# Roundings moved to GpSimd and the late layer-norm squares and variance rearranged, in a decoder layer on one core

## The chip, the core and the metric

The kernel runs on one core of a Trainium2 chip. The metric is the device time of the program in microseconds: the median of three runs. TensorE does matrix products and transposes, VectorE and ScalarE elementwise work and row reductions, GpSimd elementwise work in SBUF and part of the DMA issues, SyncE the other DMA issues. Each engine runs its own list of instructions in order and waits on semaphores for the others.

## The reference

One step of a decoder layer on a prompt of 512 tokens and 8 samples of 4 tokens, all in float32, so 544 tokens of width 1024:

```
h = rms_norm(x, g_pre)
z = h @ w_in          # 1024 x 3072: q 512 | k 256 | v 256 | ga 512 | u 512 | vs 512 | gg 512
att = block-sparse causal attention(q, k, v)     # 8 heads of 64, 4 kv heads; samples also over 1024 cached positions
v_rows = group_layer_norm(gelu(vs), g_sgu)       # 8 groups of 64: (v - mean) * rsqrt(var + 1e-5) * g
gm = gelu(u) * (tril(w_spatial[g]) @ v_rows + b) # inside chunks of 128 positions
y = x + rms_norm(concat(att * silu(ga), gm * silu(gg)) @ w_out, g_post)
```

Outputs are y, the new k and v rows, and v_rows of the samples. The variance of the layer norm is the mean of the squares of v - mean in each group of 64.

## The kernel before

All engines follow one list, `SCHEDULE`, written out by `schedule()`; each engine's program walks the list and does its part of each step. The backbone is the input projection. w_in is cut into 24 tiles of 128 columns, in the order q, k, v, vs, u, ga, gg (tiles 0-3, 4-5, 6-7, 8-11, 12-15, 16-19, 20-23); a tile is done in two halves of tokens (256 and 288), which makes 48 halves, numbered 0 to 47: step `("Z", n, half)`, half number 2n + half from tile 3 on. `("ZE", n, half)` is what is done with the result. `after(h, ...)` hangs other steps behind half h.

A product in float32 is made of three products of split values: hi x hi, hi x lo and lo x hi. A weight tile (`w_raw`, 128x1024) is rounded to its high part by ScalarE (`split_hi`, L845) and its low part, the difference, is made by VectorE or GpSimd (`split_lo`, L1094 or L718; `lo_by` says which: VectorE for tiles 7 to 12 among others). Both are issued ahead of the evacuation of the tile before: `next_split(n, 0)` is tile n + 1. TensorE waits for the high part before a tile's first half (L1541) and for the low part two thirds into it (L1546). Results of halves go alternately to two PSUM banks, and a half can't start before the bank's last result has been taken. GpSimd issues the loads of w_in tiles in pairs (`load_w_in`, L726), once both tiles that lay there have been split.

Steps that the change touches:

- `KVN tt`: TensorE turns v of token tile tt into a PSUM bank `T`; ScalarE takes it to `vn_t` (L856), rounds it to `v_st`, the high part, (L952); VectorE makes the low part (L1211); GpSimd stores `vn_t` (L771). KVN 4 is that of the samples. KVN 4 and 0 hang behind half 16, KVN 1, 2 and 3 behind 17, 20 and 22. So in GpSimd's list KVN 1 comes ahead of the step `("Z", 9, 0)`, half 18, at which tile 10 is split.
- `VSN tt`: TensorE turns gelu(vs) of token tile tt; VectorE takes the group sums (L1308) and subtracts the means (`vn`, L1310), which frees the bank; ScalarE squares (`ln_sq`, L982); VectorE adds up the squares (`ln_var`, L1313). One `ln_sq` serves all tiles in turn. VSN 3 and 4 hang behind halves 28 and 29.
- `DEX 1`: ScalarE's exponentials of the second decode round, eight of 128 columns and `p_own` (L962, L963), behind half 28 and ahead of VSN 3.
- `DOT 0`: TensorE turns the decode output and VectorE copies it in four pieces (L1299). `DPT 1`: transposes of the exponentials in two banks `T`, taken by ScalarE and VectorE (L1282).
- Halves 29, 30 and 31 (of u) have their gelu made by hand: ScalarE squares (L926), VectorE L1141, ScalarE tanh (L987), VectorE L1174 (writes `zu`, frees the bank), GpSimd halves it (L818).
- `LN`, behind half 30: VectorE makes variance + 1e-5 from the sums (L1318), shifts and subtracts for a first guess of the inverse root (L1319, L1320), GpSimd does three Newton steps (L807 to L812). `LNM`, from half 33 on: VectorE multiplies by the root, GpSimd by g_sgu.
- `PSC`, `PN`, `PS`, `PTR`, `PPV`, `ATT` u: the prompt's attention, 16 units, from half 30 on: scores, row maxima (`nmax`, L1334), exponentials (`probs`, L1000), scaling, transposes, product with v. The scores of a unit wait for the exponentials of the unit before it, as they use the same banks.

Of the kernel before, what the change touches and what calls it, by code (L numbers as in the profile page):

```python
# [39 lines left out]
ALU = mybir.AluOpType  # L40
ACT = mybir.ActivationFunctionType
# [16 lines left out]
GRP, GCH = 8, 64  # L58
# [27 lines left out]
def schedule():  # L86
# [4 lines left out]
    def after(n, *steps):  # L91
        side.setdefault(n, []).extend(steps)
# [31 lines left out]
    after(30, ("LN",))  # L124
# [77 lines left out]
def lo_by(n):  # L202

    return "pool" if n in (0, 1, 2, 5, 6) or 13 <= n <= NT else "dve"


def next_split(n, half):

    if (n, half) == (2, 1):
        return 3  # L210
    return n + 1 if half == 0 and n >= 3 else None


# [45 lines left out]
def build(nc, x_prompt, x_sample, cache_k, cache_v, page_table, g_pre, w_in, g_sgu, w_spatial,  # L259
# [13 lines left out]
    with ExitStack() as ctx:  # L273
        def sem(name):
            return ctx.enter_context(nc.semaphore(name))
# [180 lines left out]
        w_hi_done = sem("w_hi_done")  # L456
# [226 lines left out]
        def _(pool):  # L683
# [31 lines left out]
            def split_lo(n):  # L715

                pool.wait_ge(w_hi_done, split_count(n))
                nc.gpsimd.tensor_tensor(w_split_tile(False, n), w_tile(n), w_split_tile(True, n).bitcast(fp32), ALU.subtract)\  # L718
                    .then_inc(w_split["pool"], 1)
# [36 lines left out]
            for s in SCHEDULE:  # L756
# [4 lines left out]
                elif kind == "Z" and next_split(*s[1:]) is not None:  # L761
                    n = next_split(*s[1:])
                    if lo_by(n) == "pool":
                        split_lo(n)
                    if n % 2 and n + 3 < NT:
                        load_w_in((n + 3) // 2)
                elif kind == "KVN":
                    tt = s[1]
                    pool.wait_ge(t_free["act"], freed(T_FREED_BY, T_OF[s])[1])
                    if tt < 4:  # L770
                        pool.dma_start(kv_rows(v_prompt, v_sample, tt), vn_t[:, tt % 2, :]).then_inc(stored_v[tt % 2], 16)  # L771
                    else:
                        pool.dma_start(kv_rows(k_prompt, k_sample, tt), kv_s[:, 0:KVW]).then_inc(stored_kvs, 16)
                        pool.dma_start(kv_rows(v_prompt, v_sample, tt), kv_s[:, KVW:2 * KVW]).then_inc(stored_kvs, 16)
# [27 lines left out]
                elif kind == "LN":  # L802
# [27 lines left out]
        def _(act):  # L830
# [7 lines left out]
            def split_hi(n):  # L838

                w_slot_free(act, n)  # L840
                if n < 2:
                    act.wait_ge(w_first[n], 16)
                else:
                    act.wait_ge((w_in_p if w_by_pool(n) else w_in_s)[n // 2 % 2], w_load_count(n))
                nc.scalar.activation(w_split_tile(True, n), w_tile(n), ACT.Copy).then_inc(w_hi_done, 1)  # L845

            def x_stats(tt):
                R = ROWS[tt]
                act.wait_ge(x_in[tt], 16)
                link(nc.scalar.activation(x_sq[0:R, :], x_sb[0:R, tt, :], ACT.Square, accum_out=x_ss[0:R, tt:tt + 1]))  # L850
                nc.scalar.activation(x_sd[0:R, tt:tt + 1], x_ss[0:R, tt:tt + 1], ACT.Sqrt, scale=1.0 / D, bias=RMS_EPS).then_inc(x_std, 1)

# [10 lines left out]
            for s in SCHEDULE:  # L863
# [19 lines left out]
                elif kind == "Z":  # L883
# [3 lines left out]
                    if next_split(n, half) is not None:  # L887
                        split_hi(next_split(n, half))
# [51 lines left out]
                elif kind == "KVN":  # L940
# [9 lines left out]
                    if tt < 4:  # L950
                        act.wait_ge(t_free["act"], freed(T_FREED_BY, n)[1])
                        nc.scalar.activation(v_st[:, tt, :, 0:HD], vn_t[:, tt % 2, :].rearrange("p (h d) -> p h d", h=KVH), ACT.Copy)\  # L952
                            .then_inc(vst_hi, 1)
                elif kind == "DEX":
# [5 lines left out]
                    for n in range(8):  # L960
                        cs = slice(n * P, (n + 1) * P)
                        nc.scalar.activation(pd[:, cs], S[:, cs], ACT.Exp, bias=bbias[:, n // 2, n % 2:n % 2 + 1])  # L962
                    nc.scalar.activation(p_own[:, :], own_s[:, r, :], ACT.Exp, bias=nm_d).then_inc(d_exp, 1)  # L963
# [8 lines left out]
                elif kind == "VSN":  # L972
                    tt = s[1]
                    R = ROWS[tt]
                    act.wait_ge(t_free["dve"], freed(T_FREED_BY, T_OF[s])[1])
                    if tt:
                        act.wait_ge(ssq_done, tt)
                    else:
                        for n in range(2):
                            act.wait_ge(stored_v[n], 2 * 16)  # L980
                        act.wait_ge(vst_done, 4)
                    nc.scalar.activation(ln_sq[0:R, :], vn[0:R, tt, :], ACT.Square).then_inc(sq_done, 1)  # L982
# [100 lines left out]
        def _(dve):  # L1083
# [8 lines left out]
            def split_lo(n):  # L1092
                dve.wait_ge(w_hi_done, split_count(n))
                nc.vector.tensor_tensor(w_split_tile(False, n), w_tile(n), w_split_tile(True, n).bitcast(fp32), ALU.subtract)\  # L1094
                    .then_inc(w_split["dve"], 1)
# [20 lines left out]
            for s in SCHEDULE:  # L1116
# [197 lines left out]
                elif kind == "LN":  # L1314
                    dve.wait_ge(ln_made, 1)
                    dve.wait_ge(ssq_done, TT)
                    var, std, r = (t[:, :, :].rearrange("p t g -> p (t g)") for t in (ln_var, ln_std, ln_rstd))
                    link(nc.vector.tensor_scalar(var, var, 1.0 / GCH, LN_EPS, ALU.mult, ALU.add))  # L1318
# [136 lines left out]
        def _(pe):  # L1455
# [47 lines left out]
            for s in SCHEDULE:  # L1503
# [4 lines left out]
                elif kind == "Z":  # L1508
# [31 lines left out]
                    if half == 0:  # L1540
                        pe.wait_ge(w_hi_done, split_count(t))  # L1541
# [238 lines left out]
```

## Time and profile before

| | us |
|---|---|
| median of 3 runs | 280.27 (280.08 to 280.91) |
| profiled execution, its own time | 280.61 |
| its span, first to last instruction | 278.9 |
| TensorE busy | 270.3 (97%) |
| VectorE busy | 193.3 (69%) |
| ScalarE busy | 161.1 (58%) |
| GpSimd busy | 90.6 (32%) |

Busy time of TensorE is that of its matmuls, whose ends are modelled and overlap: a matmul starts before the one ahead of it ends by the record. Its clock is given as a share of full speed. In the chain of work that ended last TensorE has 82%, VectorE 8% and ScalarE 6%. Times in the text are us from the start of the span.

### The profile page before, as it was taken

How to read it: one execution, taken by the hardware profiler on the slowest of the kernel's cores; microseconds unless marked ns; L12 is line 12 of the kernel's file. 1: busy time of each engine (PE TensorE's matmuls, PEld its weight loads, DVE VectorE, ACT ScalarE, POOL GpSimd, SP SyncE). 2: the span in 40 equal slices, each digit the busy share in tenths (PEclk: the TensorE clock that was granted, in tenths of full speed). 3: DMA queues.
4: the chain of work that ended last, by engine and by line, in shares of the span. 5: the costliest groups of instructions: out<-in, count | busy, mean ns of one | idle time of the engine just before them, and what ended most of it. 6: DMA issues, size and time to landing. Idle time of an engine off the chain costs nothing.

```text
span 278.9 us, 6188 instructions
## 1 busy us (share of the span) xinstructions
PE 270.3 (97%) x2147; PEld 236.9 (85%) x2147; DVE 193.3 (69%) x460; ACT 161.1 (58%) x382; POOL 90.6 (32%) x116
## 2 busy tenths in 40 slices
PE   8999999999999999998999999999999999999992
PEld 3799998998997887997777999999998976767892
DVE  4796896699744545948756777877867794917772
ACT  5973569532692323184576587797786663628621
POOL 4576505210302042142762965443350510000000
PEclk9999999999999999999999999999999999999997
DMA  7989995469799979404464218004008404040043
GB/s 245 336 264 202 203 255 119 150 205 260 215 297 285 280 223 312 153 0 153 129 186 151 51 27 249 19 0 152 0 23 302 152 0 150 5 148 0 21 180 121
DMA packets 29986, 43.39 MB, mean 156 GB/s; under 512 B 3027, under 2 KB 22483, under 8 KB 29956
## 3 DMA queue, kind: packets, MB, share of 16 engines
q1 hardware_dynamic: 26226, 29.76, 37.7%
q0 software_dynamic: 3728, 13.24, 15.4%
q8 instruction: 17, 0.28, 0.5%
q14 instruction: 13, 0.11, 0.1%
q10 hardware_dynamic: 2, 0.00, 0.0%
HBM read 39.59 MB, written 3.41 MB: 154 GB/s over the span
## 4 chain that ended last, share of the span: by engine, by line
PE 82%; DVE 8%; ACT 6%; issue 2%; DVEq 0%; POOL 0%; ACTq 0%; POOLq 0%
PE Z L1543 12%; PE Z L1548 12%; PE Z L1544 12%; PE T L1460 5%; PE O L1684 4%; PE S L1585 3%; PE O L1620 2%; PE Z L1498 2%; PE S L1657 2%; PE S L1498 2%; PE S L1499 2%; PE Z L1500 2%; PE S L1500 2%; PE Z L1499 2%; PE S L1658 2%
## 5 line engine op out<-in xcount | busy, mean ns | idle before, releaser
L1543 PE MATMUL Z<-act_hi,w_hi 128*128 128x288 f32 (+1 forms) x344 | 89.8, 294 | 0.8 <-DVE zu L1174 0.4
L1544 PE MATMUL Z<-act_lo,w_hi 128*128 128x288 f32 (+1 forms) x344 | 88.1, 288 | 0.0
L1543 PEld LDWEIGHTS Z<-act_hi,w_hi 128*128 128x128 f32 x344 | 64.8, 188 | 3.1 <-issue 1.6
L1544 PEld LDWEIGHTS Z<-act_lo,w_hi 128*128 128x128 f32 x344 | 64.8, 188 | 0.0
L718 POOL TENSOR_TENSOR w_lo<-w_raw,w_hi 128x1024 fp32r<-128x1024 f32 x16 | 38.3, 2395 | 46.2 <-ACT w_hi L845 46.1
L1548 PE MATMUL Z<-act_hi,w_lo 128*128 128x256 f32 (+1 forms) x336 | 49.0, 288 | 0.2 <-DVE w_lo L1094 0.2
L1548 PEld LDWEIGHTS Z<-act_hi,w_lo 128*128 128x128 f32 x336 | 44.8, 188 | 0.4 <-DVE w_lo L1094 0.4
L845 ACT ACTIVATE w_hi<-w_raw 128x1024 fp32r<-128x1024 f32 x32 | 33.5, 1050 | 15.0 <-DMA w_raw<-in_w_out 9.8
L1094 DVE TENSOR_TENSOR w_lo<-w_raw,w_hi 128x1024 fp32r<-128x1024 f32 x15 | 18.9, 1268 | 16.1 <-ACT w_hi L845 16.1
L1000 ACT ACTIVATE probs<-S,nmax 128x128 f32<-128x128 f32 (+3 forms) x32 | 16.6, 524 | 21.0 <-DVE nmax L1334 20.2
L726 POOL DMA_DIRECT2D w_raw<-in_w_in x10 | 9.4, 936 | 33.1 <-DVE w_lo L1094 29.4
L1218 DVE STREAM_TRANSPOSE kT<-k_ring 128x1024 f32<-128x1024 f32 x16 | 19.8, 1236 | 0.4 <-PE S L1585 0.3
L1334 DVE TENSOR_REDUCE nmax<-S 128x1 f32<-128x128 f32 (+3 forms) x32 | 14.1, 484 | 4.4 <-PE S L1660 4.4
L1009 ACT ACTIVATE probs<-probs,rsum 128x128 f32<-128x128 f32 (+3 forms) x32 | 16.4, 573 | 0.0
L1347 DVE TENSOR_TENSOR pT_lo<-T,pT_hi 128x128 fp32r<-128x128 f32 (+3 forms) x32 | 14.2, 485 | 1.4 <-ACT pT_hi L1019 0.9
L1356 DVE TENSOR_TENSOR O<-O,o_tmp 64x128 f32<-64x128 f32 x32 | 9.5, 296 | 6.9 <-ACT o_tmp L1027 6.2
L1019 ACT ACTIVATE pT_hi<-T 128x128 fp32r<-128x128 f32 (+3 forms) x32 | 12.2, 440 | 0.5 <-PE T L1460 0.5
L1460 PE MATMUL T<-ident,probs 128*128 128x128 f32 x80 | 12.2, 278 | 0.0
L826 POOL TENSOR_TENSOR zu<-zu,zgg 128x544 f32<-128x544 f32 x4 | 5.4, 1355 | 20.5 <-DVE zgg L1185 20.5
L1684 PE MATMUL O<-pT_hi,v_st 128*128 128x256 f32 x40 | 11.6, 316 | 0.0
L922 ACT ACTIVATE zvs<-Z 128x256 f32<-128x256 f32 (+1 forms) x8 | 3.1, 398 | 13.8 <-PE Z L1548 13.8
L1657 PE MATMUL S<-k_hi,q_st 128*128 128x256 f32 (+2 forms) x32 | 10.8, 347 | 0.3 <-ACT probs L1000 0.3
(281 smaller groups left out, 561.1 us busy)
## 6 DMA issues: line engine op xcount, KB each, us to landing
w_raw<-in_w_in POOLq DMA_DIRECT2D x10, 1024.0 KB, 7.8
k_ring<-in_cache_k SPq DMA_DIRECT2D x64, 128.0 KB, 4.6
v_ring<-in_cache_v SPq DMA_DIRECT2D x64, 128.0 KB, 3.4
w_raw<-in_w_out SPq DMA_DIRECT2D x8, 512.0 KB, 4.3
x_sb<-in_x_prompt SPq DMA_DIRECT2D x4, 512.0 KB, 4.7
x_res<-in_x_prompt SPq DMA_DIRECT2D x4, 512.0 KB, 5.3
out<-y_sb SPq DMA_DIRECT2D x8, 256.0 KB, 2.0
w_raw<-in_w_in SPq DMA_DIRECT2D x2, 512.0 KB, 6.5
```

The lines of the kernel that those rows point to most:

```text
L718: nc.gpsimd.tensor_tensor(w_split_tile(False, n), w_tile(n), w_split_tile(True, n).bitcast(fp32), ALU.subtract)\
L845: nc.scalar.activation(w_split_tile(True, n), w_tile(n), ACT.Copy).then_inc(w_hi_done, 1)
L1000: ins = nc.scalar.activation(probs[:, u % 2, g, 0:keys], S[:, g * 512:g * 512 + keys], ACT.Exp, bias=nmax[:, u % 2, g:g + 1], accum_out=ps ...
L1009: nc.scalar.activation(part, part, ACT.Copy, scale=rsum[:, u % 2, g:g + 1]).then_inc(p_norm[g], 1)
L1094: nc.vector.tensor_tensor(w_split_tile(False, n), w_tile(n), w_split_tile(True, n).bitcast(fp32), ALU.subtract)\
L1218: nc.vector.transpose(kT[:, m // 2 % 2, m % 2, :, :, :].rearrange("p q a j -> p (q a j)"), k_slot(m).rearrange("p q c -> p (q c)")).then_i ...
L1460: return nc.tensor.transpose(T[n % 2][0:out_rows, col:col + rows], in_, ident[0:rows, 0:rows])
L1543: mm(out, wh[:, k, :], act_hi[:, k, cols], start=(k == 0), stop=False)
L1544: mm(out, wh[:, k, :], act_lo[:, k, cols], start=False, stop=False)
L1548: last = mm(out, wl[:, k, :], act_hi[:, k, cols], start=False, stop=(k == KD - 1))
L1657: mm(out, q, k_hi[:, kvh, 0:keys], start=True, stop=False)
L1684: last = mm(O[o_bank(u)][:, 0:256], v_st[:, j, kvh, :], part[:, u % 2, j, :, :].rearrange("p g q -> p (g q)"), start=(j == 0 and e == 0), ...
```

## The change

Five edits:

1. The rounding of v to `v_st` (step KVN) is made by GpSimd, ahead of its store, and no more by ScalarE.
2. The high part of weight tile 10 is made by GpSimd, where it splits ahead of half 18's step; VectorE's low part of that tile and TensorE wait for it. The semaphore `w_hi_done` becomes two, one for each maker, with counts by `hi_count`.
3. The square of VSN 3 is issued by ScalarE after the third of the eight exponentials of DEX 1. The others stay where they were.
4. Variance + 1e-5 is made by GpSimd (step LNV, behind half 30), no more by VectorE.
5. The guess by VectorE and the Newton steps by GpSimd (step LNG) hang behind half 31.

```diff
-    after(30, ("LN",))
+    after(30, ("LNV",))
+    after(31, ("LNG",))
+def hi_by(n):
+    return "pool" if n == 10 else "act"
+def hi_count(n):
+    return sum(hi_by(m) == hi_by(n) for m in SPLIT_ORDER[:split_count(n)])
-        w_hi_done = sem("w_hi_done")
+        w_hi_done = {"act": sem("w_hi_done_act"), "pool": sem("w_hi_done_pool")}
...
# GpSimd
                     n = next_split(*s[1:])
+                    if hi_by(n) == "pool":
+                        w_slot_free(pool, n)
+                        pool.wait_ge(w_in_p[n // 2 % 2], w_load_count(n))
+                        nc.gpsimd.tensor_copy(w_split_tile(True, n), w_tile(n)).then_inc(w_hi_done["pool"], 1)
                     if lo_by(n) == "pool":
                         split_lo(n)
...
                     if tt < 4:
+                        nc.gpsimd.tensor_copy(v_st[:, tt, :, 0:HD], vn_t[:, tt % 2, :].rearrange("p (h d) -> p h d", h=KVH)).then_inc(vst_hi, 1)
                         pool.dma_start(kv_rows(v_prompt, v_sample, tt), vn_t[:, tt % 2, :]).then_inc(stored_v[tt % 2], 16)
...
-                elif kind == "LN":
+                elif kind == "LNV":
+                    pool.wait_ge(ssq_done, TT)
+                    var = ln_var[:, :, :].rearrange("p t g -> p (t g)")
+                    nc.gpsimd.tensor_scalar(var, var, 1.0 / GCH, LN_EPS, ALU.mult, ALU.add).then_inc(ln_made, 1)
+                elif kind == "LNG":
                     pool.wait_ge(ln_guess, 1)
...
# ScalarE
+            def ln_square(tt):
+                R = ROWS[tt]
+                act.wait_ge(t_free["dve"], freed(T_FREED_BY, T_OF["VSN", tt])[1])
+                if tt:
+                    act.wait_ge(ssq_done, tt)
...
+                nc.scalar.activation(ln_sq[0:R, :], vn[0:R, tt, :], ACT.Square).then_inc(sq_done, 1)
...
-                    if tt < 4:
-                        act.wait_ge(t_free["act"], freed(T_FREED_BY, n)[1])
-                        nc.scalar.activation(v_st[:, tt, :, 0:HD], vn_t[:, tt % 2, :].rearrange("p (h d) -> p h d", h=KVH), ACT.Copy)\
-                            .then_inc(vst_hi, 1)
...
                         nc.scalar.activation(pd[:, cs], S[:, cs], ACT.Exp, bias=bbias[:, n // 2, n % 2:n % 2 + 1])
+                        if r and n == 2:
+                            ln_square(3)
...
-                elif kind == "VSN":
...
+                elif kind == "VSN" and s[1] != 3:
+                    ln_square(s[1])
...
# VectorE
-                elif kind == "LN":
-                    dve.wait_ge(ln_made, 1)
-                    dve.wait_ge(ssq_done, TT)
+                elif kind == "LNG":
+                    dve.wait_ge(ln_made, 2)
                     var, std, r = (t[:, :, :].rearrange("p t g -> p (t g)") for t in (ln_var, ln_std, ln_rstd))
-                    link(nc.vector.tensor_scalar(var, var, 1.0 / GCH, LN_EPS, ALU.mult, ALU.add))
                     link(nc.vector.tensor_scalar(std.bitcast(i32), var.bitcast(i32), 1, None, ALU.logical_shift_right))
```

## Rows read from the trace of the kernel before

**Rows 1.** Busy us of each engine by stretch, granted clock, DMA share, GB/s.

```profile
124.00:142.00 18.00, 16.46 (x143) 13.86 (x142) 11.78 (x33) 10.27 (x31) 9.85 (x18) 1.00 0.41 126
...
142.00:226.00 84.00, 84.00 (x720) 77.18 (x719) 64.09 (x202) 61.61 (x162) 39.57 (x31) 1.00 0.33 105
```

**Rows 2.** Timeline, TensorE: start, us, line, operation, [idle before <-releaser].

```profile
82.49 0.39 PE L1543 MATMUL Z<-act_hi,w_hi 128*128 128x256 f32 x1 [0.34 <-ACT zvs L922]
...
128.70 0.66 PE L1460 MATMUL T<-ident,pd 128*128 128x128 f32 x4 [0.91 <-DVE vn L1310]
...
130.43 0.40 PE L1543 MATMUL Z<-act_hi,w_hi 128*128 128x288 f32 x1 [0.37 <-DVE zu L1174]
...
135.18 0.39 PE L1657 MATMUL S<-k_hi,q_st 128*128 128x256 f32 x1 [0.26 <-ACT probs L1000]
```

**Rows 3.** Timeline, ScalarE, from 122 us.

```profile
122.48 2.18 ACT L962 ACTIVATE pd<-S,bbias 128x128 f32<-128x128 f32 x8
...
124.71 0.68 ACT L982 ACTIVATE ln_sq<-vn 128x512 f32<-128x512 f32 x1
125.23 0.46 ACT L926 ACTIVATE gelu_t<-Z 128x288 f32<-128x288 f32 x1
```

**Rows 4.** Timeline, VectorE, from 125 us.

```profile
125.42 0.69 DVE L1313 TENSOR_REDUCE ln_var<-ln_sq 128x8 f32<-128x512 f32 x1 [3.28 <-ACT ln_sq L982]
...
126.89 0.46 DVE L1141 SCALAR_TENSOR_TENSOR gelu_t<-gelu_t,Z 128x288 f32<-128x288 f32 x1
...
127.97 0.68 DVE L1310 SCALAR_TENSOR_TENSOR vn<-ln_mu,T 32x512 f32<-32x512 f32 x1
...
129.95 0.43 DVE L1174 SCALAR_TENSOR_TENSOR zu<-gelu_t,Z 128x288 f32<-128x288 f32 x1
...
131.83 2.11 DVE L1318 TENSOR_SCALAR ln_var<-ln_var 128x40 f32<-128x40 f32 x1
...
134.29 0.48 DVE L1334 TENSOR_REDUCE nmax<-S 128x1 f32<-128x128 f32 x2
```

**Rows 5.** Timeline: two tensor-scalars of VectorE, and GpSimd's low parts beside L1241 and L1318.

```profile
66.61 0.22 DVE L1241 TENSOR_SCALAR st<-off,stat 128x4 f32<-128x4 f32 x1
...
112.54 0.42 DVE L1241 TENSOR_SCALAR st<-off,stat 128x4 f32<-128x4 f32 x1
...
110.56 2.38 POOL L718 TENSOR_TENSOR w_lo<-w_raw,w_hi 128x1024 fp32r<-128x1024 f32 x1 [5.25 <-ACT w_hi L845]
...
131.50 2.40 POOL L718 TENSOR_TENSOR w_lo<-w_raw,w_hi 128x1024 fp32r<-128x1024 f32 x1
```

**Rows 6.** Timeline, ScalarE, from 78 us.

```profile
78.91 0.43 ACT L856 ACTIVATE vn_t<-T 128x256 f32<-128x256 f32 x1
...
79.70 1.05 ACT L845 ACTIVATE w_hi<-w_raw 128x1024 fp32r<-128x1024 f32 x1
```

**Rows 7.** GpSimd: two DMA issues of its timeline; groups by form (busy us, mean ns).

```profile
79.64 0.55 POOL L771 DMA_DIRECT2D out<-vn_t  x1 [3.60 <-ACT vn_t L856]
...
148.82 0.56 POOL L801 DMA_DIRECT2D out<-vn  x1 [0.29 <-POOL vn L798]
...
L818 POOL TENSOR_SCALAR zu<-zu 128x256 f32<-128x256 f32 x1 | 0.9, 851 | 0.0
...
L752 POOL TENSOR_SCALAR_AFFINE_SELECT wsp<-wsp 128x1024 f32<-128x1024 f32 x1 | 1.1, 1094 | 1.3 <-DMA wsp<-in_w_spatial 1.3
...
L809 POOL TENSOR_SCALAR ln_std<-ln_std 128x40 f32<-128x40 f32 x3 | 0.7, 225 | 0.3
...
L704 POOL TENSOR_SCALAR_AFFINE_SELECT ident<-ident 128x128 f32<-128x128 f32 x1 | 0.5, 492 | 0.2 <-POOL ind_k L699 0.2
```

**Rows 8.** Timeline: next weight load, VectorE's idle time after it, rounding of tile 14.

```profile
86.16 0.92 POOL L726 DMA_DIRECT2D w_raw<-in_w_in  x1 [5.98 <-DVE w_lo L1094]
...
93.33 1.23 DVE L1094 TENSOR_TENSOR w_lo<-w_raw,w_hi 128x1024 fp32r<-128x1024 f32 x1 [4.96 <-ACT w_hi L845]
...
109.43 1.04 ACT L845 ACTIVATE w_hi<-w_raw 128x1024 fp32r<-128x1024 f32 x1
```

More of the change, by code:

```diff
@@ L715, in split_lo @@
             def split_lo(n):
-                pool.wait_ge(w_hi_done, split_count(n))
+                pool.wait_ge(w_hi_done[hi_by(n)], hi_count(n))
                 nc.gpsimd.tensor_tensor(w_split_tile(False, n), w_tile(n), w_split_tile(True, n).bitcast(fp32), ALU.subtract)\
@@ L844, in split_hi @@
                     act.wait_ge((w_in_p if w_by_pool(n) else w_in_s)[n // 2 % 2], w_load_count(n))
-                nc.scalar.activation(w_split_tile(True, n), w_tile(n), ACT.Copy).then_inc(w_hi_done, 1)
+                nc.scalar.activation(w_split_tile(True, n), w_tile(n), ACT.Copy).then_inc(w_hi_done["act"], 1)
             def x_stats(tt):
@@ L851, in x_stats @@
                 nc.scalar.activation(x_sd[0:R, tt:tt + 1], x_ss[0:R, tt:tt + 1], ACT.Sqrt, scale=1.0 / D, bias=RMS_EPS).then_inc(x_std, 1)
+            def ln_square(tt):
[3 more added lines that the diff above has]
+                    act.wait_ge(ssq_done, tt)
+                else:
+                    for n in range(2):
+                        act.wait_ge(stored_v[n], 2 * 16)
+                    act.wait_ge(vst_done, 4)
+                nc.scalar.activation(ln_sq[0:R, :], vn[0:R, tt, :], ACT.Square).then_inc(sq_done, 1)
             def take(n, dst, src):
@@ L886, in _ @@
                     what, j, _ = ORDER[n]
-                    if next_split(n, half) is not None:
+                    if next_split(n, half) is not None and hi_by(next_split(n, half)) == "act":
                         split_hi(next_split(n, half))
@@ L971, in _ @@
                                          O[0][0:SMP, 256:256 + P].rearrange("p (c b q) -> p b c q", c=KVH, b=4), ACT.Copy).then_inc(p_own_turned, 1)
-                elif kind == "VSN":
[L973 to L982, printed above, removed]
+                elif kind == "VSN" and s[1] != 3:
+                    ln_square(s[1])
                 elif kind == "ZE" and HALF_AT[s[1], s[2]] in TANH_HALVES:
@@ L1092, in split_lo @@
             def split_lo(n):
-                dve.wait_ge(w_hi_done, split_count(n))
+                dve.wait_ge(w_hi_done[hi_by(n)], hi_count(n))
                 nc.vector.tensor_tensor(w_split_tile(False, n), w_tile(n), w_split_tile(True, n).bitcast(fp32), ALU.subtract)\
@@ L1515, in _ @@
                     if h < 3:
-                        pe.wait_ge(w_hi_done, t + 1)
+                        pe.wait_ge(w_hi_done["act"], t + 1)
                         if h == 2:
@@ L1540, in _ @@
                     if half == 0:
-                        pe.wait_ge(w_hi_done, split_count(t))
+                        pe.wait_ge(w_hi_done[hi_by(t)], hi_count(t))
                     for k in range(KD):
```

## The prediction

> **What bounds the kernel now.** I first read the busy time by stretch. TensorE is at work 84.00 of 84.00 us from 142 to 226 us, at the full granted clock, and 16.46 of 18 us from 124 to 142 us [rows 1]. So nothing that shortens another engine's work after 142 us can be seen, and the change touches the stretches before it. Next I read TensorE's own list of instructions for its idle time. Around the places that the diff touches there are four holes [rows 2]: 0.34 us ahead of 82.49 (the first matmul of weight tile 10, after ScalarE's `zvs`), 0.91 us ahead of 128.70 (second half of the transposes of the second decode round, after VectorE's `vn`), 0.37 us ahead of 130.43 (projection half 31, after VectorE's `zu`) and 0.26 us ahead of 135.18 (scores of unit 1, after ScalarE's `probs`). Together 1.88 us. That is all that the change can give back directly, 0.7% of the time. The rest is a matter of which hole closes and what new one opens.
>
> **The square of v rows, tile 3, placed after the third exponential.** ScalarE runs eight exponentials of 2.18 us from 122.48, then `p_own`, then the square at 124.71, which ends at 125.39 [rows 3]. VectorE stands idle 3.28 us until that square is done, and starts the sum at 125.42 [rows 4]. The wait is for ScalarE's order and not for data: the square follows `p_own` with no idle time. Exponentials start 0.26 us apart (2.18 less the last one's length, over seven, about), so the square now starts near 122.48 + 3 x 0.26 = 123.26 and ends near 123.94. The sum starts at 123.97, 1.45 us earlier. Behind it on VectorE are the four copies of DOT 0 and then `gelu_t` of half 29 at 126.89. That one also needs ScalarE's square of half 29, which ends at 125.23 + 0.46 = 125.69 [rows 3] and doesn't move: ScalarE does the same work in another order. So `gelu_t` goes from 126.89 to 125.74, a gain of 1.15 us, and the pair behind it, whose second half is `vn` at 127.97 to 128.65 [rows 4], ends at 127.50. TensorE wants that bank when it finishes at 128.70 - 0.91 = 127.79. The hole of 0.91 us goes, with 0.29 us to spare. What moves later is the end of the exponentials, by about 0.52 us, to 125.4 or so: TensorE asks for them only in the transposes ahead of the hole, which begin 0.6 us before 127.79. That covers it with over a microsecond.
>
> **The next hole, 0.37 us.** From the end of `vn` (128.65) to the end of `zu` (129.95 + 0.43 = 130.38) there are 1.73 us [rows 4] of ScalarE square and tanh and VectorE sum, all serial, unchanged. New end: 127.50 + 1.73 = 129.23, matmul at 129.28. TensorE would get there at 130.43 - 0.37 - 0.91 = 129.15. What is left is a hole of 0.13 us; 0.24 us are saved.
>
> **The variance made by GpSimd.** On VectorE this TENSOR_SCALAR over 128x40 takes 2.11 us, 131.83 to 133.94 [rows 4]. Its two neighbours of the same width take 0.2 us. GpSimd's `w_lo` runs from 131.50 to 133.90 beside it. The same pairing stands earlier: L1241, 128x4, takes 0.22 us at 66.61 and 0.42 us at 112.54, where it ends at 112.96, just as GpSimd's `w_lo` ends at 112.94 [rows 5]. I read both as VectorE held by GpSimd's instruction. The edit takes this operation off VectorE and puts it behind `w_lo` in GpSimd's own queue, where the same shape costs 0.22 us [rows 7], and moves the two guess operations (0.2 us each) one projection half on. VectorE then goes from the operation ahead of the variance, which let it start at 131.83 (130.7 after the shift of 1.15 us), straight to `nmax`, which stood at 134.29 [rows 4]: the row maxima come some 3.5 us earlier. ScalarE's exponentials follow, and TensorE, which gets to the scores of unit 1 at 134.92 - 1.15 = 133.77, no longer waits for them: 0.26 us saved. So 3.5 us on VectorE are worth 0.26 us at the end, since TensorE has other work until then. The Newton steps on GpSimd begin about when they did (the guess ended at 134.3 before, ahead of `nmax`; now the variance comes at about 132.9 and the guess at about 134.2, in half 31), so their reader, the normalisation in half 33, loses nothing.
>
> The Trainium skill (SBUF — State Buffer, Who interferes with whom) says that a copy or tensor_scalar of VectorE in a 2-port mode and a GpSimd instruction exclude each other for a whole instruction, whichever starts first. The two durations agree. The rule speaks against the new place too: the guess operations are still such, and GpSimd's halving of `zu` (0.85 us [rows 7]) now runs just ahead of them. By the rule VectorE could be late by up to 0.85 us there. The maxima of unit 1 wait for TensorE until about 134.7 and VectorE is there by 134.2, and a whole projection half of TensorE lies between those maxima and the transposes that need them, so the sum is the same by the rule and without it.
>
> **Weight tile 10 and v.** ScalarE loses the 1.05 us of `w_hi` at 79.70 and four roundings of v [rows 6]. `zvs`, which freed the bank for 82.49, then ends over a microsecond earlier, before TensorE is ready at 82.49 - 0.34 = 82.15 [rows 2]. TensorE now waits for GpSimd's rounding of tile 10 instead. In GpSimd's queue it stands behind the v rounding and the v store of tile 1, and these wait for ScalarE's `vn_t`, done at 79.34 [rows 6]; the store itself takes 0.55 us of issue [rows 7]. The trace of before shows no GpSimd copy. Below: a one-input GpSimd pass over 128x1024 took 1.09 us and over 128x128 0.49 us (the selects), so by the line through both 256 columns take 0.58 us [rows 7]; even a copy for nothing would give no more than the 0.34 us. Above: the TENSOR_SCALAR took 0.85 us for 256 columns [rows 7], four times that is 3.4 us for 1024. In between lies the two-input `w_lo`, 2.4 us [rows 5]. I take the nearest, the 1024-column select, since a copy also reads one input and has no scale to apply: 79.43 + 0.58, 0.29 us until a DMA instruction starts behind a computation (shown once [rows 7]; I allow up to twice that), 0.55 us of issue, then 1.1 us: 81.95 to 82.25. TensorE at 82.15: between 0.34 us gained and nothing. I enter 0.2 us. With 2.4 us it would end at 83.3 to 83.5, a hole of 1.25 us, a loss of 0.9 us.
>
> VectorE gets tile 10 about 1.3 us later; its low part is wanted 2 us behind the high part, and the K transpose, the `pdT` copy and tile 11 behind it move by 1 to 1.6 us, in front of 4.96 us of idle time that ends at 93.33. GpSimd's load of tiles 14 and 15 waits for tiles 10 and 11 and is issued about 1 us later than 86.16; ScalarE reads it at 109.43 [rows 8]. Roundings of v: VectorE's low part of v waits up to 2 us longer in KVN 0 and 2, in front of idle time each time; the stores go out 0.5 us later, and what reuses their memory, the squares, comes several stages on. I cost all these at nothing. Without the covers it would be up to 1.6 us at the next decode scores.
>
> The Trainium skill (GPSIMD Engine Reference, Engine selection) puts one-input work on GpSimd at roughly line rate and two-input work at half of VectorE's. By that page 1024 columns would be an estimated 0.85 us at its 1.2 GHz, and this hole would give the full 0.34 us, with 1.75 us in all.
>
> **Sum.** 0.91 + 0.24 + 0.26 + 0.20 = 1.61 us. The profiled execution took 280.61 us (span 278.9), 0.34 us above the median of 280.27. The sum goes off both: 279.0 for a profiled run, 280.27 - 1.6 = 278.7 us for the median. From 142 to 226 us everything is paced by TensorE, and what it gains carries through; the loads behind it are released by the work itself.
>
> **Rivals.**
> 1. The late holes close only in part: the chain behind `gelu_t` doesn't move by 1.15 us (ScalarE's square between exponentials costs more, or the halving on GpSimd holds VectorE's four copies). Then `vn` keeps some of its lateness, and 0.6 to 0.8 us are gained: 279.5 us. For it: the margins are 0.29 and -0.13 us, small. Against: each link is a duration that the trace shows.
> 2. GpSimd's copy costs what its two-input pass does: 1.41 - 0.9 = 0.5 us gained, 279.8 us. For it: rounding to the split format may be slow code. Against: the select's 1.09 us.
> 3. The slower side: GpSimd's copies run at the TENSOR_SCALAR pace. 0.85 us for v and 3.4 us for the tile end at 84.7; TensorE's hole before tile 10 is 2.6 us in place of 0.34, a loss of 2.3 us against 1.41 gained: 281.1 us. It decides from the point where the copy ends after 82.15 + 0.34 + 1.41 = 83.9 us.
> 4. The variance does not get cheap: the edit's stall was not GpSimd's hold but something at VectorE's end of the chain (its first reading of values just written). Then 2 us move to GpSimd or to the guess; TensorE still has over 2 us of slack there, and the cost is the 0.26 us at most: 279.0 us, inside the forecast.
>
> **How the numbers follow.** Forecast with rival 4: 0.64 (its own range 278.2 to 279.2, all four holes gone to all but nothing gained at tile 10). Rival 1: 0.17. Rival 2: 0.11. Rival 3: 0.08. About 0.3% (0.84 us) is what a measurement of this kernel can tell from no change, so faster means under 279.4. Rival 1 straddles that line, rival 2 lies within it. Faster: 0.64 + 0.10 = 0.74; same 0.07 + 0.11 = 0.18; slower 0.08. The range reaches from 278.0 (all 1.88 us and some noise) to 280.2, which takes in rivals 1 and 2 and leaves rival 3 out.
>
> **What would show it.** In the profile of the changed kernel: TensorE waiting neither for `vn` nor for `probs` between 124 and 137 us; the sum of tile 3 at about 124.0; the variance on GpSimd at 0.22 us and VectorE's `nmax` near 130.8; GpSimd's copy of tile 10 at 1.1 us and ended by 82.2. The prediction is wrong if that copy takes over 2 us, or if TensorE shows a new wait for `w_hi` on GpSimd of more than 0.5 us, or if holes after 142 us appear.

## The result

| | before | after |
|---|---|---|
| median of 14 runs each, same chip | 280.42 us | 278.29 us |
| lowest run | 280.02 | 277.44 |
| ratio, 95% interval | | 0.9911 (0.9891 to 0.9931) |
| profiled execution, its own time | 280.61 | 278.44 |
| its span | 278.9 | 276.7 |
| TensorE busy | 270.3 (97%) | 269.4 (97%) |
| VectorE busy | 193.3 (69%) | 192.3 (70%) |
| ScalarE busy | 161.1 (58%) | 159.1 (57%) |
| GpSimd busy | 90.6 (32%) | 93.1 (34%) |

The kernel got 0.9% faster. By the ratio that is 2.5 us (1.9 to 3.1) of 280.4; forecast were 1.6 us. The ratio counts only the undisturbed fast runs and is not the quotient of the two medians, which gives 2.1 us, inside the same interval. Taken off the 280.27 us of the forecast the ratio gives 277.8 us (277.2 to 278.3), just below the low end of the range, 278.0. The direction was right and the size too small.

The profile after, first the busy time by stretch (columns as in [rows 1]):

```profile
124.00:142.00 18.00, 17.67 (x158) 15.75 (x157) 11.26 (x38) 11.93 (x38) 11.44 (x19) 1.00 0.51 153
142.00:226.00 84.00, 84.00 (x712) 76.78 (x712) 64.78 (x200) 61.06 (x159) 38.03 (x30) 1.00 0.31 100
```

TensorE lost 1.54 us between 124 and 142 us before [rows 1]; now it loses 0.33. What it lacks is in the list of TensorE's waits (us in total, times, longest):

```profile
PE Z L1485 <- POOL warm L703: 1.4, 1, 1.4
PE T L1543 <- ACT w_hi L866: 0.4, 1, 0.4
PE Z L1563 <- DVE zu L1196: 0.3, 1, 0.3
```

The first two lie in the first 20 us, which the change doesn't touch. Of the four holes of [rows 2] one is left, that for `zu`. TensorE's timeline, around the same places:

```profile
82.26 0.27 PE L1626 MATMUL O<-ident,p_own 128*32 128x128 f32 x1
82.29 0.36 PE L1563 MATMUL Z<-act_hi,w_hi 128*128 128x256 f32 x1
...
126.99 1.03 PE L1480 MATMUL T<-ident,pd 128*128 128x128 f32 x8
127.86 0.27 PE L1626 MATMUL O<-ident,p_own 128*32 128x128 f32 x1
...
129.06 0.40 PE L1563 MATMUL Z<-act_hi,w_hi 128*128 128x288 f32 x1 [0.33 <-DVE zu L1196]
...
132.48 1.08 PE L1640 MATMUL O<-v_ring,pdT 128*32 128x258 f32 x16
133.49 0.38 PE L1677 MATMUL S<-k_hi,q_st 128*128 128x256 f32 x1
...
134.19 0.39 PE L1480 MATMUL T<-ident,probs 128*128 128x128 f32 x2
134.34 0.36 PE L1563 MATMUL Z<-act_hi,w_hi 128*128 128x256 f32 x1
```

82.29 answers to 82.49: the first matmul of tile 10 follows the one ahead of it by 0.03 us. 126.99 answers to 128.70: the eight transposes are one run and no longer two runs of four. 129.06 answers to 130.43, 133.49 to 135.18. ScalarE (answers to [rows 3] and [rows 6]):

```profile
79.28 0.43 ACT L889 ACTIVATE vn_t<-T 128x256 f32<-128x256 f32 x1
...
81.03 0.38 ACT L955 ACTIVATE zvs<-Z 128x256 f32<-128x256 f32 x1
...
122.28 0.89 ACT L991 ACTIVATE pd<-S,bbias 128x128 f32<-128x128 f32 x3
123.05 0.64 ACT L884 ACTIVATE ln_sq<-vn 128x512 f32<-128x512 f32 x1
123.58 1.41 ACT L991 ACTIVATE pd<-S,bbias 128x128 f32<-128x128 f32 x5
...
125.04 0.45 ACT L959 ACTIVATE gelu_t<-Z 128x288 f32<-128x288 f32 x1
```

The square stands between the third and the fourth exponential, 1.66 us earlier than in [rows 3]. The rounding of tile 14, the last line of [rows 8], starts at 109.23 in place of 109.43. VectorE ([rows 4], and the middle line of [rows 8]):

```profile
80.22 1.80 DVE L1233 TENSOR_TENSOR v_st<-vn_t,v_st 128x256 fp32r<-128x256 f32 x1 [2.36 <-POOL v_st L786]
...
93.13 1.23 DVE L1116 TENSOR_TENSOR w_lo<-w_raw,w_hi 128x1024 fp32r<-128x1024 f32 x1 [3.57 <-ACT w_hi L866]
...
123.72 0.69 DVE L1335 TENSOR_REDUCE ln_var<-ln_sq 128x8 f32<-128x512 f32 x1 [1.79 <-ACT ln_sq L884]
...
125.52 0.46 DVE L1163 SCALAR_TENSOR_TENSOR gelu_t<-gelu_t,Z 128x288 f32<-128x288 f32 x1 [0.35 <-ACT gelu_t L959]
...
126.60 0.68 DVE L1332 SCALAR_TENSOR_TENSOR vn<-ln_mu,T 32x512 f32<-32x512 f32 x1
...
128.57 0.43 DVE L1196 SCALAR_TENSOR_TENSOR zu<-gelu_t,Z 128x288 f32<-128x288 f32 x1
...
130.46 0.48 DVE L1354 TENSOR_REDUCE nmax<-S 128x1 f32<-128x128 f32 x2
...
131.53 0.15 DVE L1361 TENSOR_SCALAR rsum<-rsum 128x1 f32<-128x1 f32 x1
...
133.40 0.42 DVE L1339 TENSOR_SCALAR ln_std<-ln_var 128x40 int32<-128x40 int32 x1
```

The 2.11 us of L1318 are gone, and `nmax` comes at 130.46 in place of 134.29. GpSimd ([rows 5], [rows 7], first line of [rows 8]):

```profile
79.79 0.40 POOL L786 CAST v_st<-vn_t 128x256 fp32r<-128x256 f32 x1 [3.01 <-ACT vn_t L889]
80.13 0.55 POOL L787 DMA_DIRECT2D out<-vn_t  x1
80.67 1.05 POOL L777 CAST w_hi<-w_raw 128x1024 fp32r<-128x1024 f32 x1
...
86.61 0.92 POOL L737 DMA_DIRECT2D w_raw<-in_w_in  x1 [4.89 <-DVE w_lo L1116]
...
130.14 2.40 POOL L729 TENSOR_TENSOR w_lo<-w_raw,w_hi 128x1024 fp32r<-128x1024 f32 x1
132.62 0.23 POOL L822 TENSOR_SCALAR ln_var<-ln_var 128x40 f32<-128x40 f32 x1
132.93 0.85 POOL L839 TENSOR_SCALAR zu<-zu 128x256 f32<-128x256 f32 x1
```

The new operations: the copies of 0.40 and 1.05 us, the variance of 0.23 us right behind `w_lo`.

**Where the time went.** A hole in the matmul record is one measure. Another is the distance between the starts of two TensorE instructions that both kernels have, with the same work between them. I cut the profiled execution at six such starts: the first decode scores at 62.5 us, tile 10's first matmul, the transpose of `p_own` in the second round, half 31, half 32, and a product of the output projection at about 225 us. Lengths in us:

| stretch | before | after | square alone | LN alone | tile 10 and v | tile 10 alone | LN on VectorE | lo 16 on VectorE | tanh first | slow rounding | fewer edits |
|---|---|---|---|---|---|---|---|---|---|---|---|
| start to 62 us | 62.47 | 62.85 | 61.85 | 63.11 | 64.14 | 63.53 | 62.71 | 62.87 | 62.49 | 62.97 | 62.77 |
| A, to tile 10 | 20.02 | 19.44 | 20.01 | 20.02 | 19.44 | 19.44 | 19.44 | 20.01 | 19.44 | 20.81 | 19.44 |
| B, to `p_own` | 46.70 | 45.57 | 45.59 | 46.72 | 46.70 | 46.69 | 45.57 | 46.72 | 45.57 | 45.56 | 45.57 |
| C, to half 31 | 1.24 | 1.20 | 1.18 | 1.23 | 1.24 | 1.24 | 1.21 | 1.24 | 0.68 | 1.19 | 0.68 |
| D, to half 32 | 6.08 | 5.28 | 6.08 | 5.28 | 6.09 | 6.30 | 5.27 | 5.22 | 5.25 | 5.27 | 5.25 |
| to 225 us | 88.87 | 88.87 | 88.85 | 88.89 | 88.87 | 88.79 | 88.87 | 88.97 | 88.88 | 88.91 | 88.85 |

The other columns are the experiments below. Where two kernels have the same order in a stretch, their lengths mostly agree within 0.06 us (0.1 in the last one); only the first 62 us differ from execution to execution, by up to 2.3 us; why they do isn't shown. An exception is D of "tile 10 alone". This table is therefore sharper than the times of whole runs. Change from before to after: A -0.58, B -1.13, C -0.04, D -0.80, together -2.55 us; the front was 0.38 us longer in this execution, which leaves the 2.2 us between the spans. 2.55 us agree with the ratio's 2.5 (1.9 to 3.1).

### The profile page after: what moved, and what is told of

Same layout as the page of the kernel before. It is cut to its first block, busy times and chain, and to the rows that moved or that the text cites. A ratio compares the mean times of both kernels' runs of the same rounds, so it can differ in the third digit from the quotient of the medians.

```text
span 276.7 us, 6187 instructions
## 1 busy us (share of the span) xinstructions
PE 269.4 (97%) x2147; PEld 236.7 (86%) x2147; DVE 192.3 (70%) x459; ACT 159.1 (57%) x377; POOL 93.1 (34%) x122
## 4 chain that ended last, share of the span: by engine, by line
PE 84%; DMA 5%; DVE 5%; ACT 3%; issue 1%; SPq 1%; DVEq 0%; ACTq 0%
PE Z L1563 14%; PE Z L1568 13%; PE Z L1564 13%; PE T L1480 5%; DMA w_raw<-in_w_in 4%; PE O L1704 4%; PE O L1640 3%; PE S L1605 3%; PE Z L1518 2%; PE S L1677 2%; PE S L1518 2%; PE S L1519 2%; PE Z L1520 2%; PE S L1520 2%; PE Z L1519 2%; PE S L1678 2%
## 5 line engine op out<-in xcount | busy, mean ns | idle before, releaser
L866 ACT ACTIVATE w_hi<-w_raw 128x1024 fp32r<-128x1024 f32 x31 | 32.5, 1051 | 15.2 <-DMA w_raw<-in_w_out 9.9
L1116 DVE TENSOR_TENSOR w_lo<-w_raw,w_hi 128x1024 fp32r<-128x1024 f32 x15 | 18.2, 1219 | 13.6 <-ACT w_hi L866 13.6
L1518 PE MATMUL S<-w_hi,act_hi 128*128 128x512 f32 (+1 forms) x32 | 10.8, 338 | 0.0
```

The costliest lines, as they stand in the source:

```text
L1518: mm(out, act_hi[:, k, tokens(tt)], wh, start=(first and e == 0), stop=False)
```

## The experiments

Two theories stood at the start. Theory 1: the parts work as forecast, and a hole is worth more than the idle time of the matmul record says. Theory 2: the holes are worth what that record says, and the rest comes from somewhere else. The first four kernels take the change apart. Ratios are to the kernel before on the same chip, with their 95% intervals. These intervals are 1.1 us wide or more, so the whole times can't part the two theories; the stretches of the traces do.

**The square alone** (edit 3 on the kernel before).

```diff
                         nc.scalar.activation(pd[:, cs], S[:, cs], ACT.Exp, bias=bbias[:, n // 2, n % 2:n % 2 + 1])
+                        if r and n == 2:
+                            ln_square(3)
```

> The kernel before, with the third square moved between the exponentials and nothing else. Theory 1 (a hole of TensorE is worth the distance between the starts of its matmuls, which the idle time of the weight-load row shows, and not the idle time between the modelled ends of matmuls): the hole ahead of the second half of the DPT 1 transposes was worth 1.13 us, the one ahead of half 31 stays at about 0.3 us by the record; gain 1.1 to 1.2 us, 279.1 to 279.3. The scores of unit 1 still wait. Theory 2 (the idle time of the matmul record is the price, and the rest of what the change gained is something else): 0.91 us gained, 279.4 to 279.5.

Measured 279.59 us, ratio 0.9961 (0.9938 to 0.9984). B falls by 1.11 us, C by 0.06, D not at all. TensorE's and VectorE's timelines of this kernel:

```profile
128.63 0.40 PE L1562 MATMUL Z<-act_hi,w_hi 128*128 128x288 f32 x1 [0.31 <-DVE zu L1193]
...
133.38 0.38 PE L1676 MATMUL S<-k_hi,q_st 128*128 128x256 f32 x1 [0.27 <-ACT probs L1019]
```

```profile
130.03 2.11 DVE L1337 TENSOR_SCALAR ln_var<-ln_var 128x40 f32<-128x40 f32 x1
...
132.49 0.48 DVE L1353 TENSOR_REDUCE nmax<-S 128x1 f32<-128x128 f32 x2
```

The whole of B comes from the square, and the hole that follows it, for `zu`, is hardly smaller. The variance, now at 130.03, still takes 2.11 us and TensorE still waits for `probs`: the square has nothing to do with D.

**Variance and guess alone** (edits 4 and 5).

```diff
-    after(30, ("LN",))
+    after(30, ("LNV",))
+    after(31, ("LNG",))
```

> The kernel before, with the variance on GpSimd behind half 30 and the guess behind half 31, and nothing else. Theory 1: the scores, transposes and next projection half behind the first row maxima start 0.80 us earlier, 279.5. Theory 2: 0.26 us gained, 280.0. That separates the two most clearly. The holes of 0.91 and 0.37 us stay in both.

Measured 279.95 us, ratio 0.997 (0.9945 to 0.9994). D falls by 0.80 us, A, B and C stay. A hole that the record gives as 0.26 us was worth 0.80: theory 1. By the ratio the gain is 0.2 to 1.5 us, which holds the numbers of both theories.

**Tile 10 and v** (edits 1 and 2), and **tile 10 alone** (edit 2).

```diff
 def hi_by(n):
+    return "pool" if n == 10 else "act"
...
-                    if tt < 4:
-                        act.wait_ge(t_free["act"], freed(T_FREED_BY, n)[1])
-                        nc.scalar.activation(v_st[:, tt, :, 0:HD], vn_t[:, tt % 2, :].rearrange("p (h d) -> p h d", h=KVH), ACT.Copy)\
```

The removed lines (and the copy in GpSimd's list) are in the first of the two kernels only.

> The kernel before, with tile 10's high part and the roundings of v on GpSimd, and nothing else. Theory 1: the hole ahead of tile 10 closes wholly and was worth 0.59 us, 279.7. Theory 2: 0.34 us, 279.9.

> The kernel before, with tile 10's high part on GpSimd; v is rounded by ScalarE as before. Both theories: the bank for tile 10 is freed by ScalarE 1.05 us earlier and not 1.47 us, which is still before TensorE is there, and GpSimd's cast starts 0.35 us earlier, so the hole closes as in the run with both: the same time as that run within 0.1 us. If the v roundings matter by themselves (ScalarE late by 0.42 us at the bank, or VectorE's low part of v held by the cast), this run differs from it by 0.2 us or more.

Measured 280.23 us, ratio 0.9988 (0.9962 to 1.0014), and 280.06 us, 0.9963 (0.994 to 0.9986). A falls by 0.58 us in both: to hundredths the same. The rounding of v on GpSimd bought nothing. The stretches of the three partial changes add up to the whole one: 1.17 for the square (B and C), 0.80 and 0.58 make 2.55 us. Of the first kernel's whole time the ratio does not even show that it is faster. In the second kernel D is 0.22 us longer; TensorE waited 0.2 us for the scaled `probs` there (ScalarE began to scale them 0.51 us after the start of its tanh, 0.31 in the kernel before), and I have no cause for it.

**The whole layer-norm block behind half 31, on VectorE** (the changed kernel, edit 4 taken back, edit 5 kept).

```diff
-    after(30, ("LNV",))
     after(31, ("LNG",))
...
+                    dve.wait_ge(ssq_done, TT)
+                    link(nc.vector.tensor_scalar(var, var, 1.0 / GCH, LN_EPS, ALU.mult, ALU.add))
```

> The changed kernel with the variance back on VectorE, but with the whole of LN behind half 31, ahead of the guess. Theory 1 (VectorE's instruction was held by GpSimd's low part beside it, and what gains is the place): GpSimd does only its 0.85 us halving there, so the variance takes 0.2 to 0.6 us and ends before the scores of unit 1 are made; same time as the changed kernel within 0.2 us, about 277.9. Theory 2 (the variance is slow on VectorE by itself, as it reads sums just written, and GpSimd is needed for it): 2.1 us again in the new place, the maxima of unit 1 come 1.5 us late, which TensorE's half 32 partly hides; the transposes of unit 1 late, 0 to 1 us slower than the changed kernel.

Measured 278.54 us, ratio 0.988 (0.9825 to 0.9935). All stretches are those of the changed kernel. VectorE's timeline:

```profile
133.26 0.18 DVE L1334 TENSOR_SCALAR ln_var<-ln_var 128x40 f32<-128x40 f32 x1
```

At this place, behind GpSimd's `w_lo` and its halving (which ends at 133.22), the instruction that took 2.11 us takes 0.18. So edit 4 bought nothing beyond edit 5: the place was enough.

**The low part of tile 16 on VectorE** (the kernel before; GpSimd's `w_lo` beside the variance is gone, the variance stays where it was).

```diff
-    return "pool" if n in (0, 1, 2, 5, 6) or 13 <= n <= NT else "dve"
+    return "pool" if n in (0, 1, 2, 5, 6) or (13 <= n <= NT and n != 16) else "dve"
```

> The kernel before, with the low part of tile 16 made by VectorE (1.2 us) in place of GpSimd (2.4 us); nothing else. It takes GpSimd's instruction away from beside the variance. Theory 1 (the hold): the variance takes about 0.2 us in place of 2.11, the row maxima of unit 0 come about 0.7 us earlier in all, since VectorE has the 1.2 us of the low part itself. Part of the 0.80 us ahead of half 32 comes back: 0.5 to 0.8 us faster than before. Theory 2 (slow by itself): variance again 2.1 us, and 1.2 us added: 0.5 us or more slower than before.

Measured 279.77 us, ratio 0.9945 (0.9908 to 0.9983). VectorE's timeline:

```profile
131.03 1.36 DVE L1094 TENSOR_TENSOR w_lo<-w_raw,w_hi 128x1024 fp32r<-128x1024 f32 x1 [0.25 <-ACT w_hi L845]
...
133.24 0.17 DVE L1318 TENSOR_SCALAR ln_var<-ln_var 128x40 f32<-128x40 f32 x1
...
133.77 0.48 DVE L1334 TENSOR_REDUCE nmax<-S 128x1 f32<-128x128 f32 x2
```

The same instruction, with only the low part put ahead of it in VectorE's list, 0.17 us in place of 2.11: it was GpSimd's `w_lo` that held it. By itself this run leaves a gap, since the variance also reads its sums later than before. The ends close it. In the kernel before the variance ends at 133.94 and `w_lo` at 133.90; L1241 takes 0.42 us in place of 0.22 and ends at 112.96, with `w_lo` ending at 112.94 [rows 5]; in the changed kernel the first guess operation takes 0.42 us (0.18 before) and ends at 133.82, with GpSimd's halving ending at 133.78. In all three, against different instructions of GpSimd and held for very different times, VectorE is done 0.02 to 0.04 us behind GpSimd. Rival 4 falls. And D is 5.22 us, although VectorE now has tile 16's low part in it. Counted from the start of half 31 (130.84 here, 130.43 in [rows 2]) `nmax` is only 0.9 us earlier than before, and that is enough for all of D.

**Tanh ahead of the last square** (the changed kernel; on ScalarE the tanh of half 29 ahead of the square of tile 4, on VectorE `zu` ahead of that tile's sum). It goes for the hole that is left.

```diff
+                    if m == 0:
+                        ln_square(4)
...
+                        if h == TANH_HALVES[0]:
+                            ln_sum(4)
```

> The changed kernel, with ScalarE's tanh of half 29 ahead of its square of VSN 4, and VectorE's zu of half 29 ahead of the sum of VSN 4. It takes the last hole that is left there, 0.32 us by the matmul record, 0.5 us by the weight-load row, by starts about 0.4 us (a natural start at about 128.65 against 129.06). Expected 0.4 us faster than the changed kernel, about 277.5; 0.3 by the matmul record. The rival: the bank is not what half 31 waits for, and something at the same time takes its place; then no gain.

Measured 277.79 us, ratio 0.9878 (0.9825 to 0.993). TensorE and VectorE:

```profile
127.50 0.27 PE L1635 MATMUL O<-ident,p_own 128*32 128x128 f32 x1
...
128.18 0.38 PE L1572 MATMUL Z<-act_hi,w_hi 128*128 128x288 f32 x1
```

```profile
126.84 0.43 DVE L1203 SCALAR_TENSOR_TENSOR zu<-gelu_t,Z 128x288 f32<-128x288 f32 x1
```

`zu` ends at 127.27, 0.9 us before it is wanted, and C is 0.68 us, which is C without a hole. So the hole of 0.33 us in the changed kernel is worth 0.52, and that of 0.37 in the kernel before 0.56. The expectation had 0.4 us, since it put the start without a hole 0.1 us too late.

**A slow rounding** (the changed kernel, tile 10 rounded by a TENSOR_SCALAR times 1.0). It measures the price of rival 3.

```diff
-                        nc.gpsimd.tensor_copy(w_split_tile(True, n), w_tile(n)).then_inc(w_hi_done["pool"], 1)
+                        nc.gpsimd.tensor_scalar(w_split_tile(True, n), w_tile(n), 1.0, None, ALU.mult).then_inc(w_hi_done["pool"], 1)
```

> The changed kernel with GpSimd's rounding of tile 10 as a TENSOR_SCALAR times 1.0 in place of the copy; same values. It tests the price of the slower side. By the rows of before, 0.85 us for 256 columns, it takes 3 to 3.4 us and ends at 83.7 to 84.1 us (front of the changed kernel's trace). TensorE, which could start at 82.29, starts at 83.8 to 84.2: 1.5 to 1.9 us slower than the changed kernel, 279.4 to 279.8, still faster than before. VectorE's low part of v is held beside it for the whole 3 us. If the low part of tile 10 or the K transposes behind it become late too, the loss is over 2 us.

Measured 279.07 us, ratio 0.9922 (0.9891 to 0.9953). GpSimd, then TensorE:

```profile
80.81 2.82 POOL L777 TENSOR_SCALAR w_hi<-w_raw 128x1024 fp32r<-128x1024 f32 x1
```

```profile
82.38 0.27 PE L1626 MATMUL O<-ident,p_own 128*32 128x128 f32 x1
83.78 0.36 PE L1563 MATMUL Z<-act_hi,w_hi 128*128 128x256 f32 x1 [1.12 <-POOL w_hi L777]
```

2.82 us in place of 1.05; A is 1.37 us longer, where the matmul record shows a hole of 1.12. The kernel is still faster than before. The expectation missed twice: it had 1.5 to 1.9 us, from 3 to 3.4 us for the instruction, and it had VectorE's low part of v held for all of that time. That one took 1.80 us in the changed kernel and 0.43 here.

**Fewer edits** (the order of the tanh kernel, with edits 1 and 4 taken back), and then the **tanh kernel and the changed kernel again**, without an edit, all three together on one chip, to time their difference. The first one's edit on the tanh kernel:

```diff
-    after(30, ("LNV",))
...
-                        nc.gpsimd.tensor_copy(v_st[:, tt, :, 0:HD], vn_t[:, tt % 2, :].rearrange("p (h d) -> p h d", h=KVH)).then_inc(vst_hi, 1)
...
+                        nc.scalar.activation(v_st[:, tt, :, 0:HD], vn_t[:, tt % 2, :].rearrange("p (h d) -> p h d", h=KVH), ACT.Copy)\
...
+                    link(nc.vector.tensor_scalar(var, var, 1.0 / GCH, LN_EPS, ALU.mult, ALU.add))
```

> What the runs so far leave as needed: tile 10's high part on GpSimd, the third square between the exponentials, LN behind half 31 wholly on VectorE and its GpSimd steps, and tanh before square in VSN 4. The v roundings stay on ScalarE and the variance on VectorE. If the traces are read rightly these two edits bought nothing, and this kernel's shifts of TensorE against the kernel before are 0.59 us ahead of tile 10, 1.13 and 0.5 us ahead of the transposes and of half 31, and 0.80 us behind the first maxima: 3.0 us faster than before, ratio 0.989, and level with x10_tanh_again within 0.2 us. The rival: ScalarE's v rounding delays the bank for tile 10, so that the hole comes back in part, 0.2 to 0.4 us.

> The kernel of x7_tanh_first once more, beside the changed kernel on the same chip: 0.5 us faster than it, ratio 0.989 to the kernel before against 0.991.

> The changed kernel itself, on the same chip as the two others: 2.5 us faster than before, ratio 0.991 (0.989 to 0.993).

| | median of 6 | lowest | ratio | sum of A to D, less 74.04 before |
|---|---|---|---|---|
| fewer edits | 277.59 | 276.98 | 0.9914 (0.9881 to 0.9946) | -3.10 |
| tanh first | 277.98 | 276.87 | 0.9916 (0.9896 to 0.9936) | -3.10 |
| changed kernel | 278.01 | 277.84 | 0.9919 (0.9899 to 0.9939) | -2.62 |

By the sum of A to D both variants are 0.5 us shorter than the changed kernel, in each of their traces. Expected was that the whole times show it too. They don't: the medians of the two repeated kernels are 0.03 us apart. The first 62 us, in which the first weights and tokens come in, took 61.9 to 64.1 us in the traces of this study, more than the half microsecond in question. By the traces the best version is the tanh order, and of that the one with fewer edits does as well; by the whole times it isn't shown.

## Why the prediction was right in kind and short in size

The step that failed is the price of a hole: the four holes were taken at the idle time of the matmul record, 1.88 us, "all that the change can give back directly". By the distances between starts they were worth 0.58 + 1.13 + 0.56 + 0.80 = 3.07 us. The sum had 1.61 us and the stretches 2.55. Of the 0.94 us between them 0.54 are in D, 0.38 in A and 0.22 in B, and C took 0.20 back, so errors of opposite sign made the miss smaller than it was term by term.

**The hole behind the square: 0.91 forecast, 1.13 measured.** The mechanism held link by link: sum of tile 3 forecast near 124.0, found at 123.72 (123.92 by the clock of the kernel before); exponentials beside it cost nothing; the transposes run as one. Only the price was wrong. The matmul record has modelled ends that reach past the next start; two matmuls in a row overlap in it (82.26 + 0.27 against 82.29 above), and a hole is counted only from the modelled end. At tile 10 this is the whole difference: with no wait the next matmul starts 0.03 us after `p_own`, which the record has at 0.27 us, and 0.34 + 0.27 - 0.03 = 0.58. TensorE's record of its weight loads comes nearer. Its waits in the kernel before, 127 to 140 us and 80 to 90 us (us in total, times, longest):

```profile
PEld T L1460 <- DVE vn L1310: 1.1, 1, 1.1
PEld S L1657 <- ACT probs L1000: 0.7, 1, 0.7
PEld Z L1543 <- DVE zu L1174: 0.5, 1, 0.5
...
PEld T L1460 <- ACT probs L1009: 0.2, 1, 0.2
...
PEld Z L1543 <- ACT zvs L922: 0.6, 1, 0.6
```

Set beside what each hole was worth when it went (for the slow rounding, when it came):

| wait for | matmul record | weight-load record | start to start |
|---|---|---|---|
| `zvs` (A) | 0.34 | 0.6 | 0.58 |
| `vn` (B) | 0.91 | 1.1 | 1.13 |
| `zu` (C) | 0.37 | 0.5 | 0.56 (tanh first against before) |
| `probs` (D) | 0.26 | 0.7 + 0.2 | 0.80 |
| `w_hi` of the slow rounding | 1.12 | 1.4 | 1.37 |

The weight-load record is no exact price either. Loads overlap in it too, and it shows idle time where TensorE waits for nobody. Two rows at tile 10 in the slow rounding, then one ahead of the scores of unit 1 in the changed kernel:

```profile
83.75 0.19 PEld L1563 LDWEIGHTS Z<-act_hi,w_hi 128*128 128x128 f32 x1 [1.38 <-issue]
83.85 0.19 PEld L1564 LDWEIGHTS Z<-act_lo,w_hi 128*128 128x128 f32 x1
...
133.48 0.19 PEld L1677 LDWEIGHTS S<-k_hi,q_st 128*128 128x128 f32 x1 [0.41 <-issue]
```

The first is a real wait that the record doesn't put down to its maker. The last is idle time without a wait: of the 0.7 us that the kernel before shows ahead of these scores 0.4 are there in the changed kernel too, and 0.33 are the wait. That 0.7 + 0.2 comes near the 0.80 of D is in part chance. The distance between starts is the measure: by it the holes hold 3.07 us, and all of that was there to be had, as the tanh order got 3.10.

**The hole for `zu`: 0.24 forecast, 0.04 measured.** The chain was forecast well: its end at 129.23 by the clock of the kernel before. It ended at 129.00, and 129.20 when the 0.20 us that TensorE was already ahead at tile 10 are added. What was wrong is when TensorE would be there: 130.43 - 0.37 - 0.91 = 129.15. With the real prices it is 130.43 - 0.56 - 1.13 = 128.74. The same error that made the first term too small made this one too large: TensorE arrives 0.4 us earlier than the forecast had it and waits for a chain that does not.

**The variance: 0.26 forecast, 0.80 measured.** Right: 0.23 us on GpSimd, `nmax` at 130.46 (130.8 forecast), no wait for `probs`, the hold by GpSimd as the cause. Wrong in size, and for a second reason besides. The lateness of the exponentials touched several instructions of TensorE, not one. Start to start, from the product with v to half 32:

```profile
133.84 1.08 PE L1620 MATMUL O<-v_ring,pdT 128*32 128x258 f32 x16
...
136.12 0.62 PE L1460 MATMUL T<-ident,probs 128*128 128x128 f32 x2
```

From 133.84 to the scores at 135.18 [rows 2] 1.34 us, after 1.01; from the scores to the transposes 0.94, after 0.70; from the transposes to half 32 0.39, after 0.15. Three stretches longer by 0.33, 0.24 and 0.24 us, of which the prediction saw the first, at 0.26. Edits 4 and 5 were priced together, and the runs part them: moving the block (edit 5) is worth all of it, the change of engine (edit 4) nothing. The guess did run late, beside GpSimd's halving: 0.42 us at 133.40 instead of 0.18, within the 0.85 allowed and, as forecast, without cost.

The Trainium skill (SBUF — State Buffer, Who interferes with whom) has the rule that VectorE's tensor_scalar in a 2-port mode and a GpSimd instruction exclude each other for a whole instruction. The experiment with tile 16 agrees: 2.11 us beside `w_lo`, 0.17 without it. The mode itself is in no trace.

**Tile 10: 0.20 forecast, 0.58 measured.** The copy takes 1.05 us (1.1 forecast, from the select), so rivals 2 and 3 fall. Of the 0.38 us that this term was short, 0.24 are the price of the hole and 0.14 the copy's end, which was forecast too late. The copy starts earlier than the sum had it: the v rounding takes 0.40 us in place of 0.58, and the store starts at 80.13, when the rounding (79.79 + 0.40) is at its end, and not 0.29 us or more behind it; that row of [rows 7] didn't carry over. The copy ends at 81.72, or 81.34 less the 0.38 us that the front was longer; 81.95 to 82.25 was forecast. TensorE's real readiness is 82.49 - 0.58 = 81.91, so the hole goes altogether. The downstream costs entered at nothing were nothing: the next load goes out at 86.61, 86.23 less those 0.38 us, against 86.16 [rows 8], where about 1 us later was forecast, and with edit 2 alone B and C are as in the kernel before. The Trainium skill (GPSIMD Engine Reference, Engine selection) had led to an estimate of 0.85 us for the copy; the trace has 1.05, and the slow rounding, which also has one input, 2.82. The rounding of v, which had no term, is worth nothing.

**Rival 3, the slower side.** Its price is now measured in part: TENSOR_SCALAR on 1024 columns takes 2.82 us, not 3.4, and costs 1.37 us. By its stretches that kernel is 1.2 us shorter than before, by the ratio 1.3 to 3.1 us, an interval that just misses it. Even with a v rounding at 0.85 in place of 0.40 us, 0.45 us more by estimate, some 0.75 us of gain would have stayed: there was more to be had elsewhere than the rival allowed for.

**Rival 1** fell: `vn` follows in full. The range left out the time at its low end because the bound "all 1.88 us and some noise" was built on the same idle time.

## What to carry to other kernels

Price a hole of TensorE by the distance between two starts against a stretch of the same work without a hole, and not by the idle time between matmuls. The wait in its weight-load record is a second look, less what that record shows there with nothing to wait for. Look behind the one instruction that shows a wait for smaller ones on its neighbours. When one hole closes, TensorE arrives earlier by its full price at the next one, so the next term must be worked out with that price too. When an instruction of VectorE takes ten times its usual time beside a GpSimd instruction, try another place for it first: here that was enough, and another engine added nothing.

## What the runs showed of the hardware

- GpSimd's CAST from f32 to fp32r takes 1.05 us for 128x1024 and 0.40 us for 128x256. TENSOR_SCALAR on the same 128x1024 takes 2.82 us, and one from f32 to f32 on 128x256 0.85 us. The form of the instruction, with the same result, makes a factor of 2.7.
- GpSimd's `w_lo` held VectorE's TENSOR_SCALAR of 128x40 and of 128x4 until it ended, and one of 128x1 not: in the changed kernel `rsum` took 0.15 us at 131.53, beside a `w_lo` from 130.14 to 132.54, and `zu` at 131.99 its usual 0.42. That the size decides isn't shown.
- VectorE's low part of v, 128x256 with two inputs, takes 1.80 us at 80.22 in the changed kernel, where GpSimd's copy of tile 10 follows, and 0.43 us ahead of the TENSOR_SCALAR of the slow rounding. Nine traces have that copy or its slow form. In eight of them VectorE's instruction took 1.70 to 1.80 us and ended 0.3 us behind the copy's end; the ninth is the slow form. Why the slow form lets it through isn't shown; there VectorE's instruction ends (80.76) before GpSimd's starts (80.81), while in the changed kernel it would, at 0.43 us, have ended at 80.65, before the copy starts at 80.67. The Trainium skill (SBUF — State Buffer, Who interferes with whom) says that a VectorE instruction with two inputs in SBUF contends with a GpSimd instruction that reads there; the 1.80 us agree with that, the starts alone don't explain it.
